# Stacked high and low parts in the attention, the bias added on VectorE, and a second expert slot of 64 rows

## What is computed

```python
scores = einsum(qc, kb) * d ** -0.5               # mixer A: 8 heads of 64, all earlier chunks of 64 tokens
scores = where(valid, scores + bias, NEG_INF)     # bias: learned, by clipped distance
probs  = softmax(scores); out = probs @ vb
# mixer B: 8 query heads on 2 key heads, own and previous chunk, ALiBi penalty, a learned sink in the softmax
merged = gates[0] * (ya @ w_branch_a) + gates[1] * (yb @ w_branch_b); x += merged @ w_out
x += swiglu(h)              # layer 0, dense
x += sum of top 2 of 8 experts, combine[e] * swiglu(h, w_gate[e], w_up[e], w_down[e])   # layer 1
```

## Time and profile before

| what | us |
|---|---|
| median of 3 runs | 1946.87 |
| lowest and highest run | 1941.91 and 1948.41 |
| span of the profiled execution | 1947.5 |
| PE busy in it | 1846.8 (95%) |
| DVE, ACT, POOL busy | 998.9, 845.3, 78.9 |
| mean granted TensorE clock | 0.974 |

### The profile page before, as it was taken

How to read it: one execution, slowest core, us unless ns; L and a number is a source line. 1 busy time by engine, 2 the same in 40 slices (tenths; PEclk the granted TensorE clock), 3 DMA queues, 4 the chain that set the end, 5 groups by cost and what they waited for, 6 DMA issues and landing times.

```text
span 1947.5 us, 23957 instructions
## 1 busy us (share of the span) xinstructions
PE 1846.8 (95%) x8476; PEld 1471.9 (76%) x8477; DVE 998.9 (51%) x1579; ACT 845.3 (43%) x1348; POOL 78.9 (4%) x106
## 2 busy tenths in 40 slices
PE   7999999999999999999999999989999999999993
PEld 5877777777888878878677777748888777788882
DVE  5335555555333333353355555464545788875555
ACT  4234454233323222232344442344444787764543
POOL 0000000000000000000000000030000011110002
PEclk9989999999999999999899999999999999999997
DMA  4322111222333323323211112155767899986664
GB/s 145 97 70 52 38 43 34 66 86 69 96 97 98 97 89 100 92 80 97 62 41 47 33 44 76 54 202 155 207 178 208 300 345 332 346 313 191 185 194 177
DMA packets 76357, 255.04 MB, mean 131 GB/s; under 512 B 12000, under 2 KB 12000, under 8 KB 75760
## 3 DMA queue, kind: packets, MB, share of 16 engines
q1 hardware_dynamic: 71056, 239.16, 38.7%
q0 software_dynamic: 5216, 14.76, 2.5%
HBM read 245.48 MB, written 10.52 MB: 131 GB/s over the span
## 4 chain that ended last, share of the span: by engine, by line
PE 85%; DVE 6%; ACT 3%; issue 3%; DMA 1%; SPq 0%; ACTq 0%; DVEq 0%; POOL 0%; POOLq 0%; PEldq 0%
PE ps L1104 17%; PE ps L1105 15%; PE ps L1106 15%; PE ps L1373 8%; PE ps L1375 8%; PE ps L1374 8%; PE ps L1231 2%; PE ps L1238 2%; PE ps L1234 2%; PE ps L1217 2%; ACT m_hi L700 1%; DVE m_lo L1026 1%; PE ps L1259 1%; PE ps L1258 1%; ACT w_hi L516 1%
## 5 line engine op out<-in xcount | busy, mean ns | idle before, releaser
L1026 DVE TENSOR_TENSOR m_lo<-m_raw,m_hi 128x1024 fp32r<-128x1024 f32 (+1 forms) x285 | 327.7, 1164 | 215.1 <-ACT m_hi L700 212.0
L1104 PE MATMUL ps<-h_hi,w_hi 128*128 128x512 f32 x1008 | 417.6, 414 | 12.5 <-DVE h_lo L917 8.1
L772 DVE TENSOR_TENSOR w_lo<-raw,w_hi 128x1024 fp32r<-128x1024 f32 x166 | 201.3, 1213 | 433.2 <-ACT w_hi L516 433.2
L1105 PE MATMUL ps<-h_lo,w_hi 128*128 128x512 f32 x1008 | 398.0, 395 | 0.0
L1106 PE MATMUL ps<-h_hi,w_lo 128*128 128x512 f32 x1008 | 397.5, 394 | 0.0
L700 ACT ACTIVATE m_hi<-m_raw 128x1024 fp32r<-128x1024 f32 (+1 forms) x285 | 284.2, 1011 | 230.0 <-PE ps L1375 226.0
L516 ACT ACTIVATE w_hi<-raw 128x1024 fp32r<-128x1024 f32 x166 | 173.8, 1047 | 391.6 <-PE ps L1106 391.0
L1104 PEld LDWEIGHTS ps<-h_hi,w_hi 128*128 128x128 f32 x1008 | 191.8, 190 | 69.1 <-issue 13.6
L1106 PEld LDWEIGHTS ps<-h_hi,w_lo 128*128 128x128 f32 x1008 | 191.8, 190 | 42.0
L1373 PE MATMUL ps<-m_hi,xt_hi 128*128 128x512 f32 (+1 forms) x576 | 218.6, 379 | 5.1 <-issue 2.0
L1374 PE MATMUL ps<-m_lo,xt_hi 128*128 128x512 f32 (+1 forms) x576 | 216.5, 376 | 0.0
(11 more groups left out here) (212 smaller groups left out, 2422.7 us busy)
## 6 DMA issues: line engine op xcount, KB each, us to landing
m_raw<-moe_g SPq DMA_DIRECT2D x135, 512.0 KB
m_raw<-moe_down SPq DMA_DIRECT2D x88, 512.0 KB
raw<-w_in SPq DMA_DIRECT2D x68, 512.0 KB, 3.7
m_raw<-moe_g SPq DMA_DIRECT2D x64, 384.0 KB
raw<-w_gu SPq DMA_DIRECT2D x44, 512.0 KB, 3.7
raw<-w_out SPq DMA_DIRECT2D x16, 512.0 KB, 3.6
raw<-w_down SPq DMA_DIRECT2D x16, 512.0 KB, 3.5
raw<-w_a SPq DMA_DIRECT2D x8, 512.0 KB, 3.6
```

The source lines that it names most:

```text
L772: V.tensor_tensor(lo, raw[:, n % RAW, 0:cols], hi.bitcast(F32), ALU.subtract).then_inc(lo_ready, 1)
L1026: V.tensor_tensor(m_lo[:, u % M_SPL, 0:cols], m_raw[:, u % M_RAW, 0:cols], m_hi[:, u % M_SPL, 0:cols].bitcast(F32), ALU.subtract).then_inc ...
L1104: E.matmul(ps[:, bank, :], wh, hi, start=first, stop=False)
L1105: E.matmul(ps[:, bank, :], wh, lo, start=False, stop=False)
```

## The change

The attention keeps stacked operands. `q_both` holds for each head its high part on 64 partitions and its low part on the other 64; `k_hi` and `k_lo` hold a head's keys on both halves of the partitions, the second half copied by POOL's DMAs. Two matmuls of 128 rows give all four products. `v_both` has a head's values as 64 columns of high and 64 of low parts, so that the output comes in two halves that DVE adds. The bias is reversed once a head by a float32 matmul, biased on ACT into `bias_t`, and added by DVE in the instruction that also takes the (negated) maximum. A finished head goes: ACT moves one half, DVE adds, ACT high part, DVE low part.

In the experts the second slot has 64 rows: 64 columns of high and 64 of low parts in `xt_both` and `at_both`, two matmuls per product, and the halves of the result are moved by ACT and added by DVE after each chunk's gate, each chunk's up, and at the end. `CAP` is 192, further rounds are two (16 visits), with 48 lists in place of 32. Cut to its core (POOL, ScalarE, VectorE and TensorE in the attention, then the same three in the experts):

```diff
-CAP = SLOTS * P
-HALVES = T // CAP
-LISTS = HALVES * EXPERTS * SLOTS
+TAIL = P // 2
+CAP = P + TAIL
+ROUNDS = -(-T // CAP)
+LISTS = ROUNDS * EXPERTS * SLOTS
...
+            def double_keys(layer):
+                for u in K_UNITS:
+                    pool.wait_ge(drained_dve, layer * N_PROJ + u + 1)
+                    for own, hi, lo, other in halves(u):
+                        pool.dma_start(hi[other, :], hi[own, :]).then_inc(k_doubled, 16)
+                        pool.dma_start(lo[other, :], lo[own, :]).then_inc(k_doubled, 16)
...
-                    A.activation(kq_hi[:, u, :], ps[:, n % 2, :], ACT.Copy,
-                                 scale=SCALE if 4 <= u < 12 else 1.0).then_inc(kq_hi_ready, 1)
+                    for own, hi, _, _ in halves(u):
+                        A.activation(hi[own, :], ps[own, n % 2, :], ACT.Copy,
+                                     scale=SCALE if 4 <= u < 12 else 1.0).then_inc(kq_hi_ready, 1)
...
-                        A.activation(kq_hi[r:r + HD, st["q"], :], ps[r:r + HD, O_BANK + hh % 2, :],
-                                     ACT.Copy).then_inc(y_hi_ready, 1)
+                        A.activation(y_other[r:r + HD, :], ps[HD - r:P - r, O_BANK + hh % 2, :], ACT.Copy).then_inc(y_moved, 1)
+                    if tick >= 9 and tick % 4 == 1:
+                        A.wait_ge(y_added, H + 1)
+                        A.activation(y_tiles(hh)[0][r:r + HD, :], y_sum[r:r + HD, :], ACT.Copy).then_inc(y_hi_ready, 1)
...
-                            V.tensor_reduce(stat[:, 1, c:c + 1], sc[:, 0:nk], AX.X, ALU.max, negate=True).then_inc(nmax_ready, 1)
+                        V.tensor_tensor_reduce(out=sc[:, 0:nk], in0=sc[:, 0:nk], in1=bias_t[:, H % 2, T - nk:], scale=-1.0,
+                                               scalar=-MASKED if st["a"] else nsink[:, layer, st["head"]:st["head"] + 1],
+                                               op0=ALU.add, op1=ALU.min, accum_out=stat[:, 1, c:c + 1]).then_inc(nmax_ready, 1)
...
+                        V.tensor_tensor(y_sum[r:r + HD, :], ps[r:r + HD, O_BANK + hh % 2, :], y_other[r:r + HD, :],
+                                        ALU.add).then_inc(y_added, 1)
...
+                def turn_bias(hh, bank):
+                    i = layer * HEADS + hh
+                    E.wait_ge(bias_masked, i + 1)
+                    E.matmul(ps[:, bank, 2 * P:], flip[:], bias, start=True, stop=True).then_inc(bias_turned, 1)
...
-                        E.matmul(out, q_hi, k_hi, start=True, stop=False)
-                        E.matmul(out[:, nk - near:nk], flip_r[:], bias_hi[:, H % 2, 2 * P - near:2 * P], start=False, stop=False)
-                            E.matmul(out[:, nk - near:nk], flip_r[:], bias_lo[:, H % 2, 2 * P - near:2 * P], start=False, stop=False)
-                        E.matmul(out, q_hi, k_lo, start=False, stop=False)
-                        E.matmul(out, q_lo, k_hi, start=False, stop=True).then_inc(scores_ready, 1)
+                        E.matmul(out, q, hi[:, k0:k0 + nk], start=True, stop=False)
+                        E.matmul(out, q, lo[:, k0:k0 + nk], start=False, stop=True).then_inc(scores_ready, 1)
...
-                                E.matmul(out, v_hi[:, kt, vc], p_hi, start=j == 0, stop=False)
-                                E.matmul(out, v_hi[:, kt, vc], p_lo, start=False, stop=False)
-                                mm = E.matmul(out, v_lo[:, kt, vc], p_hi, start=False, stop=j == len(products) - 1)
+                                E.matmul(out, v_both[:, kt, v, :], p_hi, start=j == 0, stop=False)
+                                mm = E.matmul(out, v_both[:, kt, v, :], p_lo, start=False, stop=j == len(products) - 1)
...
 +                                if u == CHUNK_END[c]["up"] and slots > 1:
+                                    moved(1, ps[TAIL:P, 3, 0:w])
...
+                                        V.wait_ge(tail_moved, i * T_MOVES + (moves0 + 2 * c + 2))
+                                        V.tensor_tensor(m_act[0:TAIL, 1, 0:w], ps[0:TAIL, 3, 0:w], m_other[:, 1, 0:w],
+                                                        ALU.add).then_inc(tail_up, 1)
+                                        V.tensor_tensor(m_act[0:TAIL, 1, 0:w], m_silu[0:TAIL, 1, 0:w], m_act[0:TAIL, 1, 0:w],
+                                                        ALU.mult).then_inc(m_act_ready, 1)
...
+                            if sl:
+                                E.matmul(out, both[:, x, :], wh, start=start, stop=False)
+                                return E.matmul(out, both[:, x, :], wl, start=False, stop=stop)
```

More of the change, by code:

```diff
@@ L252, in step @@
             k0 = max(qb - 1, 0) * P
-            return dict(hh=hh, qb=qb, a=False, q=8 + j, k=12, rows=HD * g, v=4, head=j + 4 * g,
+            return dict(hh=hh, qb=qb, a=False, rows=HD * g, v=HEADS + g, head=j + 4 * g, keys=(kb_hi[:, g, :], kb_lo[:, g, :]),
                         k0=k0, nk=(qb + 1) * P - k0)
@@ L458, in where_used @@
                 with pool.If(pool.value_load(used[0], min_val=0, max_val=T) > used[1]):
-                    move(P)
+                    move(rows)
                 with pool.Else():
@@ L604, in _ @@
                         A.wait_ge(pT_ready, s + 1)
+                        if st["qb"] == 0 and st["hh"] < 2 * HEADS - 1:
+                            bias_tile(layer * 2 * HEADS + st["hh"] + 1, T_BANK + s % 2)
                         if s >= 4:
@@ L712, in _, with passes, moved @@
             turned_x(0, 1)
-            def passes(first, always_both):
-                with A.Fori(0, N_SEC) as i:
+            def passes(first, sections, always_both):
+                with A.Fori(0, sections) as i:
                     def pass_of(slots):
+                        def moved(half, of):
+                            A.activation(m_other[:, half, 0:of.shape[1]], of, ACT.Copy).then_inc(tail_moved, 1)
                         for u in range(M_UNITS):
@@ L984, in _ @@
             V.tensor_tensor(r1[:, 2, :], r1[:, 1, :], r1[:, 0, :], ALU.subtract).then_inc(gap_ready, 1)
-            rank, col, row, past1, past2, past3, times, col0 = (spot[:, j, :] for j in range(8))
+            rank, col, row, past1, past2, past3, past4, tails, rounds, col0 = (spot[:, j, :] for j in range(10))
             link(V.tensor_tensor(of_both_e, both, twice_e.unsqueeze(1).to_broadcast([P, 2, TT, EXPERTS]), ALU.mult))
@@ L1039, in _, with passes @@
             turned_x(0, 1)
-            def passes(first, always_both):
-                with V.Fori(0, N_SEC) as i:
+            def passes(first, sections, always_both):
+                with V.Fori(0, sections) as i:
                     def pass_of(slots):
+                        moves0 = T_MOVES * first
                         for u in range(M_UNITS):
                             for c in range(len(CHUNKS)):
+                                w = CHUNKS[c] * P
+                                if u == CHUNK_END[c]["gate"] and slots > 1:
+                                    V.wait_ge(tail_moved, i * T_MOVES + (moves0 + 2 * c + 1))
+                                    V.tensor_tensor(m_silu[0:TAIL, 1, 0:w], ps[0:TAIL, 1, 0:w], m_other[:, 0, 0:w],
+                                                    ALU.add).then_inc(tail_summed, 1)
```

348 lines of the change are left out of this document (199 added, 149 removed).

## The result

The changed kernel takes 1806.23 us (median of 4 runs, 1804.19 to 1808.75) against 1944.39 for the kernel before on the same chip: ratio 0.928, 95% interval 0.926 to 0.930. The forecast was 1817, in a range of 1775 to 1862. The profiled execution spans 1803.8 us.

The account below looks back on a forecast made before the run. PE bound attention and two-slot experts; in attention the ACT and DVE chain would take over. From 1947.5 us: attention -85.6, +2.6 and +2.8 around it, experts -59.8 and +8.8, +1: -130.2, so 1817, range 1775 to 1862.

Parts of the forecast that it names:

- What the PE needs: Attention: the PE's work alone would take 10.1 us for a head of A and 8.8 for one of B.
- The chain in mixer B: ACT's weight split to the PE's transposes, 4.3 us: PE idle 1.8 and 0.7, a head 11.0 us, saved 2.25.
- The chain in mixer A: The same ACT and DVE chain ends at 6.0 us against PE work 4.6: a head 11.5 us, saved 3.1.
- the slow rival: Attention: gaps keep TensorE's clock low all through, heads 20.2 and 17.6 us, +159, total 2060 us; chance 0.03.
- the 1.4 at the end: Attention's end: the last head has one move and one add more, 1.4 us a layer, +2.8.
- The add-and-minimum: Attention, DVE: the fused operation equals today's maximum, 0.42 us at 256 columns, plus 0.15 to read the accumulated value.
- the second rival: Attention: add-and-minimum takes twice as long or ACT and DVE meet more often, 19 to 32 us, 1836 to 1850; chance 0.17.
- a stall of 2.2: Two-slot experts: PE waits for the second slot's sums, 0.45 us twice and 1.3 at the third chunk; +8.8 in all.
- the cover at the chunks' ends: Two-slot experts: 10 matmuls and four transposes, 2.7 us, hide part of the second slot's 3.2 us chain.
- The last scatter: Experts' end: the last add before the scatter costs +0.5 us.
- The chain is hidden: Attention: DVE runs far enough ahead and the PE stays the bound, -143 us there, total 1751; chance 0.12.
- the chain eats all: Experts: the second slot's chain costs what it saves, a two-slot expert keeps 95 us, +51, total 1868; chance 0.07.

Follow-up runs that it names:

- the experiment with 64 rows: Kernel before, with the bias's reversing matmuls on 64 rows instead of 128: 1903.61 us, ratio 0.978.
- The kernel with both moves: Changed kernel, attention's weight split later in the head, and second slot's half moved before ACT's split at up chunks' ends: 1768.26 us, ratio 0.909.
- The whole move: Changed kernel, attention's weight split and finished head's low part on later ticks, ACT's copy of that head's half ahead of the gate: 1778.48 us, ratio 0.914.

## Why the prediction was right, point by point

**What the PE needs.** Forecast 10.1 us for a head of A and 8.8 for one of B. Idle time taken off the period, it is 10.78 - 4.64 / 6 = 10.0 (six heads from 148.60) and 10.72 - 13.95 / 7 = 8.7. My own terms for A add up to 14.58 - 3.7 - 0.65 - 0.5 + 0.6 = 10.3 and not to 10.1, and the parts of a head of B to 8.8 + 1.8 + 0.7 = 11.3 and not to 11.0; the forecast would have been some 5 us higher by the latter. Scores without changes of rows, 0.5 us: measured 0.55, and the experiment with 64 rows shows the 0.2 us a change behind it. The reversing matmul, put at 0.6, holds the PE from 195.37 to 195.90, 0.53.

**The chain in mixer B** was right in mechanism, links and size: 4.3 us, a wait of 1.6 where 1.8 stood, then 0.7, and in every other head 1.3 and 0.35; 10.72 where 11.0 stood.

**The chain in mixer A** was sized too long: 11.5 forecast, 10.65 measured. The wait that I put at 1.4 us is 0.77 a head: the largest miss within the steady heads, 0.85 us times 16, 14 us. The timeline of a head of A, from the split to the reversing matmul that stands before the transposes:

```profile
191.60 1.05 ACT L574 ACTIVATE w_hi<-raw 128x1024 fp32r<-128x1024 f32 x1
...
194.49 0.41 DVE L935 CUSTOM_DVE_ANT_0 ps<-ps,bias_t 128x256 f32<-128x256 f32 x1
...
195.37 0.70 PE L1296 MATMUL ps<-norm,flip 128*128 128x256 f32 x2 [0.61 <-DVE probs L949]
```

The chain is 3.8 us there, where I had taken the 4.3 of mixer B over: its add-and-minimum is shorter (0.41 against 0.49) and no sum with the sink's term stands before the scaling.

**The first head.** I had saved 3.1 us on it as on any other; it went from 18.2 (126.43 to 144.62) to 10.9 (127.74 to 138.65). Some 4 us a layer more than forecast, and the clock's stretch of 4.4 us is about that: the profile of the kernel before has it in both layers, that of the changed kernel in neither. I saw the stretch and used it only for the slow rival, never as time that the kernel before already paid. Over all profiles 9 of 10 starts with the old attention have one and 3 of 16 with the new, so these 8 us of the two layers go with the change, but by a way that no term of the forecast had; why it is so is open. Heads and first head together: 7 x 0.85 + 8 x 0.28 + 4.2 = 12.4 a layer, against -53.7 measured and -41.4 forecast (42.8 less the 1.4 at the end), a gap of 12.3.

**The add-and-minimum.** 425 ns in A, as the 417 of the nearest row said, and 487 in B, where it also takes the sink as an operand; the read of the accumulated value 127 ns, put at 150. The Trainium skill, Vector Engine (DVE) Microarchitecture Reference, Points that are easy to get wrong, has a two-source operation (`S2S2D2_STT`) at half its throughput when both sources are non-bf16 in SBUF. Here one source is in PSUM, so the rule would not slow it, and 425 against 417 ns agrees; whether the fused operation is of that kind no run shows. The size was right, but what hung on it was not: the second rival took an operation 0.27 us slower than forecast, counted it two or three times a head, and came to 0.6 to 1 us a head, 19 to 32 us. Taking it apart adds 0.3 to 0.4, counts four times a head, and costs 1.5 and 1.8 a head, 54 in all.

**The experts.** 15.0 us saved an expert and a stall of 2.2, so -12.8; measured 95.90 - 84.67 = 11.2, so a stall of 3.8. The term that was undersized is the cover at the chunks' ends: I counted ten matmuls of 0.227 us and four transposes, 2.7 us, at both. After the second up chunk the ten are 384 wide, 1.76 us from the first to the transposes (1250.77 to 1252.53), a cover shorter by 0.5; the PE waits 0.67 us after the first chunk of that expert and 0.89 after the second. The groups by form show both places, the transposes and the down product:

```profile
L1470 PE MATMUL ps<-m_hi,at_both 128*128 128x512 f32 x88 | 34.7, 394 | 6.4 <-DVE m_act L1141 6.4
...
L1482 PE MATMUL ps<-ident,m_act 128*128 128x128 f32 x132 | 20.9, 283 | 15.9 <-DVE m_act L1132 9.2 <-DVE m_act L1141 6.2
```

6.2 / 4 = 1.55 us an expert at the transposes, where 0.9 stood, and 6.4 / 4 = 1.6 at the third chunk, where 1.3 stood. The rest, 0.6, is not placed. Single-slot experts stayed at 52.6 to 54.3, as forecast.

**The last scatter** was put at +0.5 and costs +3.3 us:

```profile
1765.90 1.01 ACT L812 ACTIVATE y_stage<-ps 128x1024 f32<-128x1024 f32 x1
1766.93 1.02 ACT L815 ACTIVATE m_other<-ps 64x1024 f32<-64x1024 f32 x1
...
1767.98 1.22 DVE L1157 TENSOR_TENSOR y_stage<-ps,m_other 64x1024 f32<-64x1024 f32 x1 [0.73 <-ACT m_other L815]
...
1771.00 0.93 POOL L543 DMA_INDIRECT y_dram<-y_stage,lists  x1 [2.26 <-issue]
```

From the first copy to the second scatter's issue 5.10 us where it was 3.34: the add (1.22) is in series behind the move, and I had counted only what it exceeds a copy by. The remaining 1.5 lies between the scatter and the first use of its rows. Projections, +1.3 a layer, came as forecast.

**The sum.** Attention 24.7 us better than forecast, experts, routing and scatter 8 worse, projections as forecast, the end of the span 2.6 that nobody had counted: 1804 in place of 1817 for the profiled execution. That the forecast lay within 1% is in part luck: errors of 24.7 one way and of 11 the other, and some 8 of the 24.7 are the clock's stretches, which no term had. For the experts alone the forecast was too low a time.

**The rivals.** "The chain is hidden" (1751) is excluded by the PE's waits, "the chain eats all" (1868) by the expert periods, the clock that stays low by 1.00 in the windows. Its mechanism does exist in a small way: with longer waits in every head of B, the run with add and maximum apart fell to 0.50 for 3.4 us in nine of its heads. The kernel with both moves reaches 1768, close to the 1751 of the first rival: most of what that rival described can be had by where the steps stand.

## What to carry to other kernels

When a stage's PE work is cut by a third, the place of long ACT and DVE operations in the repeating schedule becomes the bound. After such a change, move each long operation to the tick in which nothing on the path follows it, and let DVE use what ACT makes one tick later, not in the same tick: the second is worth 18 us by itself here. The whole move was worth 28 us of 1806 in the new kernel, and one like it 7 in the old, with no work removed. Where a sum crosses engines, make the move that starts the chain the first thing that ACT does at the stage's end, and count the cover with the width of the matmuls that really follow.

## What the runs showed of the hardware

- A change between 64-row and 128-row operands costs the PE 0.2 us, whether it goes up or down: in the tick with 512 keys three changes stand for 1.52 - 0.91 = 0.6 us and one for 0.2. 32 heads with two changes fewer a tick (256 in all) were worth 41 us; the rest of the 51 went into the waits of mixer B.
- Stretches at a granted clock of 0.50 (1.2 GHz) follow the idle time before the attention in 9 of the 10 starts profiled with the old attention (five profiles, two layers each), and in 3 of 16 with the new (eight profiles). The PE waits 1.28 and 1.41 us in both before it starts. The stretches last from some 3 to 10 us. The second execution of the kernel before had one start of each kind, so the order of the work alone does not decide. What does is open.
- A VectorE operation with a per-partition operand besides its two sources takes 487 ns at 256 columns where the same without takes 425.
- Behind VectorE's last operation, the kernels with the new attention take 5.8 us to the end of the span, the others 3.2; the attention part alone has it (5.8), the experts alone do not (3.2). The trace's records of the sequencers, which the views leave out, place it on GpSimd: its closing DRAIN ends 8.0 us behind its last operation in the first group and 4.8 in the second, and in the first group it ends last of all engines' drains. The new attention also brings GpSimd 40 DMA issues more (97 against 57); that these are the cause was not tested.
